# Expert weights: eight pieces requested ahead of the loop over rounds, each round requesting the next one's, and gathered rows placed in the high parts' buffers

## What is computed

```
h2 = rms_norm(x, norm2_g) * (1 + sc2) + sh2
g_idx  = argmax(h2 @ w_group + b_group)              # one of 4 groups
top_i  = top 2 of the 4 experts of that group
y = 0
for e in range(16):
    ff = (silu(h2 @ w1[e]) * (h2 @ w3[e])) @ w2[e]   # 1024 -> 512 -> 1024
    y = y + combine[:, e] * ff                       # zero where the token did not take e
x = x + gt2 * y
```

## Time and profile before

| | |
|---|---|
| median of 3 runs | 1626.55 us |
| lowest and highest | 1623.75 and 1627.8 us |
| the profiled execution's own time | 1624.66 us |
| its span, first to last instruction | 1622.8 us |
| PE busy | 1505.1 us (93% of the span) |
| DVE busy | 816.6 us (50%) |
| ACT busy | 651.5 us (40%) |
| POOL busy | 357.5 us (22%) |
| data moved | 290.31 MB, 179 GB/s on the mean |
| loads through the ring of the experts | 188 of 512 KB |

### The profile page before, as it was taken

The page is one execution under the profiler, slowest core; times in us unless marked ns, Lnnn a source line. Parts: engine busy times, 40 slices in busy tenths (PEclk is TensorE's granted clock), DMA queues, the critical chain, the costliest instruction groups (busy, mean ns, idle before and its releaser), DMA issues.

```text
span 1622.8 us, 21317 instructions
## 1 busy us (share of the span) xinstructions
PE 1505.1 (93%) x7820; PEld 1127.1 (69%) x7820; DVE 816.6 (50%) x1391; ACT 651.5 (40%) x1069; POOL 357.5 (22%) x197
## 2 busy tenths in 40 slices
PE   5999999999999999999989899999999799999981
PEld 3774777477747774777767677677788578877771
DVE  3332341234123412221875767643265699988984
ACT  5312311221123112312435354544223378888871
POOL 1341133122312231223331112111422100000002
PEclk9999999999999999999999999999999699999995
DMA  9424452445244523432431253145740799999975
GB/s 347 163 65 142 153 194 63 134 153 196 66 130 153 196 66 130 143 105 81 158 117 53 69 179 130 40 157 199 217 124 26 240 312 394 394 389 385 389 297 207
DMA packets 158091, 290.31 MB, mean 179 GB/s; under 512 B 15083, under 2 KB 40859, under 8 KB 157733
## 3 DMA queue, kind: packets, MB, share of 16 engines
q1 hardware_dynamic: 154246, 278.47, 50.0%
q0 software_dynamic: 3744, 10.49, 1.7%
HBM read 251.55 MB, written 40.52 MB: 180 GB/s over the span
## 4 chain that ended last, share of the span: by engine, by line
PE 29%; DMA 9%; DVE 8%; issue 3%; ACT 2%; SPq 1%; POOL 0%; DVEq 0%; ACTq 0%; POOLq 0%
PE pj L93 7%; PE pj L95 7%; PE pj L94 7%; DMA m_raw<-w 6%; DVE d_tmp L2192 2%; PE d_B L2464 1%; PE d_B L2483 1%; PE d_B L2491 1%; DMA ring_raw<-w_out 1%; PE d_B L2525 1%; ACT m_hi L1394 1%; PE d_B L2473 1%; DMA d_kc<-cache_diff_k 1%; PE d_B L1569 1%; DMA ring_raw<-w_br_diff 1%
## 5 line engine op out<-in xcount | busy, mean ns | idle before, releaser
L93 PE MATMUL pj<-ring_hi,hT_hi 128*128 128x512 f32 x880 | 369.4, 420 | 7.0 <-DVE hT_lo L689 3.1
L95 PE MATMUL pj<-ring_hi,hT_lo 128*128 128x512 f32 x880 | 346.0, 393 | 0.0
L94 PE MATMUL pj<-ring_lo,hT_hi 128*128 128x512 f32 x880 | 345.1, 392 | 0.0
L479 POOL TENSOR_TENSOR ring_lo<-ring_raw,ring_hi 128x1024 fp32r<-128x1024 f32 x79 | 191.7, 2428 | 544.4 <-ACT ring_hi L545 544.4
L545 ACT ACTIVATE ring_hi<-ring_raw 128x1024 fp32r<-128x1024 f32 x79 | 83.4, 1059 | 418.8 <-DMA ring_raw<-w_in 354.9
L1473 DVE TENSOR_TENSOR m_lo<-m_raw,m_hi 128x1024 fp32r<-128x1024 f32 x188 | 223.8, 1221 | 26.1 <-ACT m_hi L1394 23.4
L93 PEld LDWEIGHTS pj<-ring_hi,hT_hi 128*128 128x128 f32 x880 | 166.6, 189 | 61.3 <-issue 29.2
L1394 ACT ACTIVATE m_hi<-m_raw 128x1024 fp32r<-128x1024 f32 x188 | 194.6, 1058 | 28.4 <-DMA m_raw<-w 26.5
L95 PEld LDWEIGHTS pj<-ring_hi,hT_lo 128*128 128x128 f32 x880 | 166.0, 189 | 37.1
L94 PEld LDWEIGHTS pj<-ring_lo,hT_hi 128*128 128x128 f32 x880 | 167.0, 190 | 28.5 <-issue 1.0
L1923 POOL TENSOR_TENSOR ring_lo<-ring_raw,ring_hi 128x1024 fp32r<-128x1024 f32 x37 | 91.6, 2478 | 315.5 <-ACT ring_hi L1943 315.5
(11 more groups left out here) (341 smaller groups left out, 2384.8 us busy)
## 6 DMA issues: line engine op xcount, KB each, us to landing
m_raw<-w SPq DMA_DIRECT2D x188, 512.0 KB, 10.8
ring_raw<-w_in SPq DMA_DIRECT2D x72, 512.0 KB, 3.6
r_S<-state_ret SPq DMA_DIRECT2D x64, 256.0 KB, 4.5
r_ada_raw<-w_ada SPq DMA_DIRECT2D x16, 1024.0 KB, 7.0
o_state_s<-r_S SPq DMA_DIRECT2D x64, 256.0 KB, 4.7
a_raw<-w_ada SPq DMA_DIRECT2D x8, 1024.0 KB, 12.1
ring_raw<-w_in SPq DMA_DIRECT2D x32, 256.0 KB, 3.2
ring_raw<-w_br_ret SPq DMA_DIRECT2D x16, 512.0 KB, 4.1
```

Source lines behind the costliest of these rows:

```text
L93: pe.matmul(out, s_hi, m_hi, start=start, stop=False)
L94: pe.matmul(out, s_hi, m_lo, start=False, stop=False)
L95: return pe.matmul(out, s_lo, m_hi, start=False, stop=stop)
L479: pool.tensor_tensor(lo[:, p], raw[:, p], hi[:, p].bitcast(F32), ALU.subtract).then_inc(lo_done, 1)
```

## The change

The diff in full:

```
+AHEAD = range(4, 12)
...
-        self.gx = [[row(f"gx{a}_{t}", at[a * NT + t]) for t in range(NT)] for a in range(2)]
         hi_at = [wt + 16384 + 4096 * i for i in range(4)] + [base + 16384] + [base + 71680 + 4096 * i for i in range(4)] \
             + [base + 20480 + 4096 * i for i in range(3)]
         self.hi = [piece(f"hi{i}", hi_at[i], F32R) for i in range(RING)]
+        self.gx = [[row(f"gx{a}_{t}", hi_at[a * NT + t]) for t in range(NT)] for a in range(2)]
...
+    def load(self, sp, n):
+        sp.dma_start(self.raw[self.slot(n)][:], self.source(n)).then_inc(self.loaded[self.slot(n)], 16)
+
     def run_sp(self, sp):
         io = self.io
         R = self.rounds(sp)
         with sp.Fori(0, R) as r:
-            for n in range(4, PIECES):
+            for n in range(AHEAD.stop, PIECES):
                 e = (n - 28) // 12
                 if n >= 28 and (n - 28) % 12 == 0:
                     self.send_y(sp, r, e)
-                if n == 8:
+                if n == AHEAD.stop:
                     sp.wait_ge(*self.rows_in(r, 0))
                 if n - RING >= 4:
                     sp.wait_ge(*self.piece_used(r, n - RING))
-                sp.dma_start(self.raw[self.slot(n)][:], self.source(n)).then_inc(self.loaded[self.slot(n)], 16)
+                self.load(sp, n)
             for e in range(N_EXP - 2, N_EXP):
                 self.send_y(sp, r, e)
+            for t in range(NT):
+                sp.wait_ge(self.gath[t], r * 32 + 32)
+            for n in AHEAD:
+                self.load(sp, n)
             for t in range(NT):
                 sp.wait_ge(*self.added(r, t))
                 out = io["o_y_p"][0, t * P:(t + 1) * P] if t < NP_T else io["o_y_s"].rearrange("b l d -> (b l) d")
                 sp.dma_start(out, self.K.x1[:, t]).then_inc(self.out, 16)
             sp.wait_ge(self.out, r * (NT * 16) + NT * 16)
+            for n in AHEAD:
+                each = 16 * len(range(n, PIECES, RING))
+                sp.wait_ge(self.loaded[self.slot(n)], r * each + each + 16)
             sp.sem_inc(self.stored, 1)
...
             for t in range(NT):
                 sp.wait_ge(h2_done, 2 * t + 2)
                 sp.dma_start(io["xg"][t * P:(t + 1) * P], K.h2[:, t]).then_inc(moe.h2_out, 16)
+                if t >= NP_T - 1:
+                    sp.wait_ge(w_done, 2 * NT)
+                    for n in AHEAD[4 * (t - NP_T + 1):4 * (t - NP_T + 2)]:
+                        moe.load(sp, n)
```

## The result

The change makes the kernel slower. The median is 1634.93 us (1629.25 to 1638.49, 12 runs) against 1625.63 us (1622.86 to 1628.13, 12 runs) for the kernel before, run beside it: a ratio of 1.0059 with a 95% interval of 1.0049 to 1.0069, or +9.3 us by the medians. The forecast was +7.6 us.

What follows compares the result with a forecast made beforehand. DMA was taken to bound the experts' stage from 1340 to 1570 us, by a little, but not before; behind 1589 the end hangs on DVE and the last store. Front 0, end +7.6: 1626.55 + 7.6 = 1634.2 us, range 1631.3 to 1638.1.

Steps and rivals of the forecast that it cites:

- Front: loads 4 to 11 moved up: Start of the experts' stage: all twelve buffers are full at 1295.6 us either way, so earlier loads gain 0.
- The bound on the side of gain: Experts' stage: at most 10.7 us gained, all eight loads at 1.33 us, if DMA-bound from its first moment.
- An earlier start of PE: First turning of gathered tokens: expert 0's gather may land sooner, but PE gets there no sooner; 0.
- What is moved past what: SP's queue before the experts: moved loads fit ahead of tile 4's store and SP's next duty; 0, loss bound 1 us.
- gx in the high parts' buffers: Final gathers: they wait as before for the last two results' stores, with same sizes and order; 0.
- The end: After the experts: gathers' wait, then eight unneeded loads ahead of five output stores; +7.6 us, range +4.7 to +11.5.
- the front pays 10.7 us: Rival, experts' stage: eight transfers less remove PE's idle time, last piece 10.7 us sooner, 1623.5 us; chance 0.13.
- the tail is hidden: Rival, kernel's end: loads and stores run beside each other, only the last load counts; +0.9, 1627.5 us; chance 0.09.
- in part: Rival, kernel's end: stores overlap loads in part; between +1 and +4.7, 1628 to 1631 us; chance 0.07.

Runs made afterwards that it cites:

- Front only: The changed kernel without its second asking: pieces 4 to 11 still loaded ahead of the loop, nothing loaded at the end of a round; ratio 0.9991, median 1625.15 us.
- loads later: The kernel before with pieces 4 to 7 also waiting for the gathered tokens of expert 0; ratio 0.9992, median 1625.11 us.
- the one large relief: The kernel before with eight neighbouring pieces (52 to 59) loaded as 32 KB instead of 512 KB, computation same in amount; ratio 0.9985, median 1622.83 us.
- the spread relief: The kernel before with eight pieces loaded as 32 KB instead of 512 KB, two at every second expert; ratio 0.9951, median 1617.55 us.
- end only: The changed kernel's end (gathers' wait, eight extra loads before the output's stores) with the front of the kernel before; ratio 1.0061, median 1635.49 us.
- the two kernels with small pieces: The kernel before with eight pieces loaded as 32 KB instead of 512 KB, in one place (ratio 0.9985) or two at every second expert (0.9951).
- the one with four loads: The changed kernel with four extra loads at the end instead of eight; ratio 1.0032, median 1631.66 us.

## Why the prediction was right

**Front: loads 4 to 11 moved up, taken at 0.** Right, and by its own reason. The step was that the ring is full at the moment when piece 16 is asked for, with either kernel. In the changed kernel that piece was asked for 14.2 us behind the turning of tokens (14.8 before), and pieces 16 to 19 landed as in the earlier trace rows:

```profile
L1333 SPq DMA_DIRECT2D m_raw<-w x4: 368/368/373, 1298.7 to 1302.8; - x4
...
DMA to landing us min/median/max: 3.3/3.3/3.3
```

The stretches say where the saved time went: behind the turning of tokens the DMA share fell from 0.92 to 0.57, and from 14 us behind it on share and rate were as before. Front only (0.9991) shows no gain beyond 0.2%, loads later (0.9992) that the start has slack on the other side too, and the one large relief (0.9985) that most of what DMA saves while the ring is full is idled away. The bound on the side of gain, 10.7 us, was of the right order for that amount of DMA, only not at this place: the spread relief brought 8.0 us by the ratio (4.7 to 11.4).

**An earlier start of PE, taken at 0.** Right: 76.68 us from the first store of h2 to the turning of tokens, 76.69 before. **What is moved past what, taken at 0.** Right: the four loads behind tile 3's store were issued in 1.9 us and the store of tile 4 was not late; gt2's loads ended at 1268.9, some 5.5 us ahead of SP's next duty, the old kernel's 1270.7 shifted by the 3.7 us of the table. **gx in the high parts' buffers, 0.** Right: front only has it, and shows no price.

**The end, taken at +7.6.** The mechanism was right and the size 1.7 us short (9.3). Against the last result's store, the working had the wait for the gathers over at +20.95 us, and it was over at +21.3 us. It had the eighth load landed 12.6 us later; it took 14.2. That is the term that was mis-sized: I had spaced the loads by the 1.33 us of a running stream, and a batch that starts on an idle queue doesn't run like one. It had five stores at 1.33 us; they took 6.2 us together, 1.24 each. The last 0.3 us lie behind the last landing, where SP now has eight more semaphores to wait for; that these are the reason was not tested. So 7.6 + 0.3 + 1.6 - 0.5 + 0.3 = 9.3. From the last store's issue to its landing the end is 11.6 us instead of 2.6.

The forecast of the median, 1634.2 us, is only 0.7 us from the measured 1634.93, though the term is 1.7 us short. That is luck: the kernel before measured 0.9 us less in the comparison (1625.63) than in the three runs that the forecast started from (1626.55).

**The rivals.** That the front pays 10.7 us is refuted by front only and end only; a gain below 0.2% is not. That the tail is hidden, in part or wholly, loads and stores passing each other, is refuted by the changed kernel's own rows: no store landed in less than 10.4 us. The prediction named the wait for the last load only in the rival of the hidden tail, at +0.9 us. It costs whatever stands behind the loads: with the stores first the end was dearer still (+12.0), for SP closes the round by waiting for them.

## What to carry to other kernels

A prefetch into a ring that is full by the time of its first use bought nothing, though the stage behind it is DMA-bound for most of its length: ask at which moment a buffer is free that would otherwise be filled too late, and take or move transfers there. That small portions do better than one large one is what the two kernels with small pieces suggest, not what they prove. A prefetch for the next turn of a loop is paid in the last turn as well, where nobody needs it; put it where the queue has room (here some 20 to 40 us earlier, as buffers fell free: +9.3 us became nothing measurable), never between the last compute and the output's stores. And before a gain in one trace is put down to the change, split PE's time into idle and busy: here 4.0 of 10.5 us were the same matmuls in less time.

## What the runs showed of the hardware

A batch of 512 KB loads that starts on an idle queue sags after its first two or three loads. In the end of the kernel with eight extra loads and the old front, DMA's rate in slices of 0.5 us, from 1608 to 1628 us (the loads begin at 1610.4):

```profile
GB/s 418 369 123 25 0 0 25 66 369 389 402 418 377 160 229 315 315 332 356 381 385 385 393 406 410 406 365 393 385 389 430 414 406 434 410 451 401 401 442 410
```

After 2.5 us at 370 to 418 GB/s it falls to 160, and is back above 380 only 3 us later. The changed kernel's end (a fall to 115) and the one with four loads (a fall to 111 and some 3.5 us below 300) show the same. In single transfers it is one hole: the second load lands at 1615.3 us and the third at 1618.6, where the others land 1.2 to 1.5 us apart. It is not peculiar to the end of the kernel. The loads that the changed kernel asks for at 1251.8 and 1261.7 us fall to 188 and 172 GB/s, and the ring's first loads in the kernel before fall to 135, the latter two with other transfers beside them; only behind the stores, in the kernel that sends those first, is the dip shallow (225). Against 3.3 us and 1.33 for each further load, eight loads at the end took 1.6 us more in the changed kernel and four took 2.4 us more, so the loss belongs to the batch and not to its size. That is what my expectation of +3 us for four loads lacked (+4.9). The cause is open; nothing here tells whether it is the place of the data in memory, the issuing, or the engines.
